# A hybrid state-space and attention layer on one core: early stages rebuilt around TensorE's queue, GpSimd adds squares, the scan spread

## What is computed

```python
mod = silu(c) @ w_ada + b_ada                 # shift1, scale1, gate1, shift2, scale2, gate2
hn = rmsnorm(x, norm_mix_pre) * (1 + sc1) + sh1
z, xbc, dt, q, k, v, gates = split(hn @ w_in)
y_ssm = grouped_rmsnorm(scan(silu(conv(xbc)), dt) * silu(z))       # 8 groups, chunked scan
y_att = attention(rope(q), rope(k), v)        # window of 128, 64 queries at a time, learned sinks
merged = sigmoid(g_ssm) * (y_ssm @ w_ssm_out) + sigmoid(g_att) * (y_att @ w_att_out)
x = x + g1 * rmsnorm(merged @ w_out, norm_mix_post)
gate, up = split((rmsnorm(x, norm_ffn_pre) * (1 + sc2) + sh2) @ w_ffn_in)
x = x + g2 * rmsnorm((silu(conv(gate)) * up) @ w_ffn_out, norm_ffn_post)
```

## Time and profile before

| | us |
|---|---|
| median of 3 runs | 1462.64 (1460.32 to 1465.84) |
| the profiled execution | 1468.68 |
| its span, first to last instruction | 1466.9 |
| stage A and the start of stage B, to the end of chunk 1 | 0 to 79.2 |
| the rest of stage B | 79.2 to 238.9 |
| the group loop | 238.9 to 709.3 |
| what follows | 709.3 to 1466.9 |
| TensorE busy | 1365.2 (93% of the span) |
| VectorE, ScalarE, GpSimd busy | 772.5, 502.6, 405.6 |

### The profile page before, as it was taken

How to read it: one execution, slowest core, us unless ns; L and a number is a source line. 1 busy time by engine, 2 the same in 40 slices (tenths; PEclk the granted TensorE clock), 3 DMA queues, 4 the chain that set the end, 5 groups by cost and what they waited for, 6 DMA issues and landing times. The chain is left out here.

```text
span 1466.9 us, 24764 instructions
## 1 busy us (share of the span) xinstructions
PE 1365.2 (93%) x10355; PEld 1269.8 (87%) x10355; DVE 772.5 (53%) x1288; ACT 502.6 (34%) x888; POOL 405.6 (28%) x263
## 2 busy tenths in 40 slices
PE   4699998999999999999899999994899999999994
PEld 1488987898898998988889999993899999999993
DVE  1644414877887888778353000328566666650114
ACT  2212424363553553634323222333333333322221
POOL 0532310101101011011123444331444444443332
PEclk7599987999999999999999999996799999999997
DMA  9276624344245343341333222221222222222221
GB/s 373 101 259 223 198 77 120 104 127 141 70 136 147 89 123 116 118 131 45 113 119 132 87 87 87 101 82 38 74 87 87 87 87 87 87 74 91 88 68 62
DMA packets 68351, 165.83 MB, mean 113 GB/s; under 512 B 21160, under 2 KB 34376, under 8 KB 64768
## 3 DMA queue, kind: packets, MB, share of 16 engines
q1 hardware_dynamic: 68240, 164.25, 34.7%
HBM read 150.85 MB, written 13.83 MB: 112 GB/s over the span
## 5 line engine op out<-in xcount | busy, mean ns | idle before, releaser
L181 PE MATMUL psum<-hp_hi,w_hi 128*128 128x274 f32 x1488 | 458.7, 308 | 15.9 <-POOL hp_lo L298 11.7
L159 POOL TENSOR_TENSOR w_lo<-raw_w,w_hi 128x1024 fp32r<-128x1024 f32 x127 | 307.0, 2418 | 569.8 <-ACT w_hi L153 569.8
L181 PE MATMUL psum<-hp_lo,w_hi 128*128 128x274 f32 x1488 | 438.6, 295 | 0.0
L181 PE MATMUL psum<-hp_hi,w_lo 128*128 128x274 f32 x1488 | 438.1, 294 | 0.0
L153 ACT ACTIVATE w_hi<-raw_w 128x1024 fp32r<-128x1024 f32 x175 | 185.1, 1058 | 629.4 <-PE psum L181 576.5
L181 PEld LDWEIGHTS psum<-hp_hi,w_hi 128*128 128x128 f32 x1488 | 287.8, 193 | 35.7 <-issue 16.4
L181 PEld LDWEIGHTS psum<-hp_lo,w_hi 128*128 128x128 f32 x1488 | 290.7, 195 | 0.8
L181 PEld LDWEIGHTS psum<-hp_hi,w_lo 128*128 128x128 f32 x1488 | 288.9, 194 | 0.0
L181 PE MATMUL psum<-hq_hi,w_hi 128*128 128x274 f32 x832 | 248.1, 298 | 15.4 <-POOL hq_lo L1568 13.3
L181 PE MATMUL psum<-hq_hi,w_lo 128*128 128x274 f32 x832 | 244.9, 294 | 0.0
L181 PE MATMUL psum<-hq_lo,w_hi 128*128 128x274 f32 x832 | 244.6, 294 | 0.0
(11 more groups left out here) (235 smaller groups left out, 2018.9 us busy)
## 6 DMA issues: line engine op xcount, KB each, us to landing
raw_w<-in_w_grp SPq DMA_DIRECT2D x57, 512.0 KB, 3.8
raw_w<-in_w_ffn_in SPq DMA_DIRECT2D x44, 512.0 KB, 3.6
ada<-in_w_ada SPq DMA_DIRECT2D x12, 1024.0 KB, 20.3
ada_g<-in_w_ada SPq DMA_DIRECT2D x6, 2048.0 KB, 8.6
raw_w<-in_w_ffn_out SPq DMA_DIRECT2D x22, 512.0 KB, 3.5
acs_b<-mem_acs SPq DMA_DIRECT2D x8, 1096.0 KB, 7.1
raw_w<-in_w_ssm SPq DMA_DIRECT2D x16, 512.0 KB, 3.5
raw_w<-in_w_qkv SPq DMA_DIRECT2D x13, 512.0 KB, 6.7
```

The source lines that it names most:

```text
L159: eng.tensor_tensor(flat(w_lo[self.hl_slot(n)]), raw_w[self.raw_slot(n)][:], flat(w_hi[self.hl_slot(n)]).bitcast(F32), ALU.subtract).then_ ...
L181: mm = pe.matmul(out[:, h, :], w, x[:, cols], start=first and j == 0, stop=last and j == 2)
```

## The change

Stage A. BLOCKS is now SHIFT1, SCALE1, SHIFT1 + 1, SCALE1 + 1, so that two blocks are enough for the first four tiles; the two blocks of SHIFT2 move to stage B. x is loaded first, in two halves, into mr (which is free then). After the sum, VectorE norms (`normed`) and makes hp_lo (`lower`) and w_lo; ScalarE scales and shifts (`scaled`) and makes hp_hi; GpSimd only clears constants. TensorE multiplies chunks 0 and 1 tile by tile between the blocks 2 and 3. The tables cos, sin, rot, gp and mask_u, chunks 3 and 4 of the weights and the block GATE1 are loaded at the end of stage A.

```diff
-                for t in range(2):
+                for t in range(len(src)):
                     mm = pe.matmul(psum[0:SUMW, bank, col + j:col + j + 1], src[t][:, c0:c0 + SUMW], ones[:, 0:1],
-                                   start=t == 0, stop=t == 1)
+                                   start=t == 0, stop=t == len(src) - 1)
...
+        MOD_BLOCKS = [GATE1, GATE1 + 1, SCALE2, SCALE2 + 1, SHIFT2, SHIFT2 + 1, GATE2, GATE2 + 1]
...
+            BLOCKS = [SHIFT1, SCALE1, SHIFT1 + 1, SCALE1 + 1]
+            ada = [ada_g1, *(sb(st, f"ada{n}", [P, KB, ADA_W]) for n in range(1, len(BLOCKS)))]
+            mod_row = late_row
+            x = mrg
...
+                    for n in range(2):
+                        ks = slice(KB // 2 * n, KB // 2 * (n + 1))
+                        sp.dma_start(x[:, ks, :], i["x"][:, ks, :]).then_inc(in_x[n], 16)
...
                         if n == 4:
-                            sp.dma_start(x[:], i["x"]).then_inc(in_x, 16)
+                            w.load(sp, 0)
+                            w.load(sp, 1)
...
-                        if a >= ADA_SLOTS:
-                            sp.wait_ge(ada_done, a - ADA_SLOTS + 1)
-                        sp.dma_start(ada[a % ADA_SLOTS][:, ks, :], i["w_ada"][BLOCKS[a], :, ks, :]).then_inc(in_ada[n], 16)
-                    for n in range(RAW_SLOTS):
-                        w.load(sp, n)
+                        sp.dma_start(ada[a][:, ks, :], i["w_ada"][BLOCKS[a], :, ks, :]).then_inc(in_ada[n], 16)
+                    w.load(sp, 2)
+                    for dst, name in ((cos, "cos"), (sin, "sin"), (rot, "rot"), (dt_par, "dt_par"), (gp_all, "gp"), (mask_u, "mask_u")):
+                        sp.dma_start(dst[:], i[name]).then_inc(in_s, 16)
+                    w.load(sp, 3)
+                    w.load(sp, 4)
+                    sp.wait_ge(ada_done, 1)
+                    sp.dma_start(ada_g1[:], i["w_ada"][MOD_BLOCKS[0]]).then_inc(ada_in[0], 16)
...
+                    def scaled(t):
+                        act.wait_ge(gain_s, t // 4 + 1)
+                        act.wait_ge(xr_s, t + 1)
+                        if t >= 2:
+                            act.wait_ge(lo_s, t - 1)
+                        for c0, L, g in RANGES:
+                            ins = act.activation(h[t % 2][:, c0:c0 + L], xr[t % 2][:, c0:c0 + L], ACT.Identity,
+                                                 bias=mod[:, t, g:g + 1], scale=gain[:, 0, t, g:g + 1])
+                        ins.then_inc(h_s, 1)
+                        act.wait_ge(h_s, t + 1)
+                        act.activation(hp_hi[:, t, :], h[t % 2][:], ACT.Copy).then_inc(hi_s, 1)
...
+                    act.activation(halves(rstd[:]), slot(1), ACT.Sqrt, bias=eps_c, scale=1.0 / D).then_inc(root_s, 1)
+                    row(0)
+                    row(1)
+                    w.split_hi(act, 0)
+                    act.wait_ge(const_s, 3)
+                    scaled(0)
+                    scaled(1)
+                    w.split_hi(act, 1)
+                    scaled(2)
+                    scaled(3)
+                    row(2)
+                    row(3)
+                    for t in range(4, KB):
+                        scaled(t)
+                    w.split_hi(act, 2)
...
+                    def normed(t):
                         if t >= 2:
...
+                            dve.wait_ge(h_s, t - 1)
+                        dve.tensor_tensor(xr[t % 2][:], x[:, t, :], rstd[:], ALU.mult).then_inc(xr_s, 1)
+
+                    def lower(t):
+                        dve.wait_ge(hi_s, t + 1)
+                        dve.tensor_tensor(hp_lo[:, t, :], h[t % 2][:], hp_hi[:, t, :].bitcast(F32), ALU.subtract).then_inc(lo_s, 1)
+
+                    normed(0)
+                    gains(0)
+                    normed(1)
+                    w.split_lo(dve, 0)
+                    for t in range(2, KB):
+                        lower(t - 2)
+                        normed(t)
+                        if t == 3:
+                            w.split_lo(dve, 1)
+                        if t == 5:
+                            gains(1)
+                    lower(KB - 2)
+                    lower(KB - 1)
+                    w.split_lo(dve, 2)
+                    dve.wait_ge(lo_s, KB)
...
+                    for a in range(2):
+                        turn_block(a)
+                    first_chunk(0)
+                    first_chunk(1)
+                    block_product(2)
+                    first_chunk(2)
+                    first_chunk(3)
+                    turn_block(2)
+                    second_chunk(0)
+                    block_product(3)
+                    second_chunk(1)
+                    second_chunk(2)
+                    turn_block(3)
+                    second_chunk(3)
+                    for k in range(4, KB):
+                        first_chunk(k)
+                        if k == KB - 2:
+                            second_chunk(4)
+                    for k in range(5, KB):
+                        second_chunk(k)
+                    w.block = 2 * KB
...
+                            if n == AT + 3:
+                                sp.wait_ge(v_s, 2)
...
+                                load_attention(sp, at.in_s, S, at.q, scratch["qs"], scratch["ks"], scratch["vs"][0:WIN, :], scratch["vs"][WIN:WIN + S, :],
...
+                            if n - 4 in MOD_AT[0:6]:
+                                load_ada(sp, (2, 3, 4, 5, 7, 6)[MOD_AT.index(n - 4)])
...
-                            w.split_hi(act, n + 2)
                             if n == AT + 1:
                                 at.exps(act, 0)
+                            if n >= 1:
+                                w.split_hi(act, n + 2)
...
+                                    at.evac_turned(act, 0, 2)
                                 if n == AT + 2:
-                                    at.evac_turned(act, 0, 2)
...
-                                if n == AT + 1 and k == 1:
+                                if n == AT + 1 and k == 2:
                                     pe.wait_ge(tok_s, 1)
-                                    pe.wait_ge(row_s, 6)
...
+                                    pe.wait_ge(row_s, 8)
+                                if n == AT + 1 and k in (2, 4):
+                                    for kv in (k - 2, k - 1):
                                         at.scores(pe, 0, kv)
-                                u = (n - AT - 2) * KB + k - 3
+                                u = (n - AT - 2) * KB + k - 6
...
+                                if u == 8:
+                                    for a in range(2):
+                                        mm = turn_rows(pe, 6, 8 * a, late_row[:, 2 + a, :])
+                                    mm.then_inc(turn_s, 1)
+                            for j in (() if n < 2 or n > QK else (0, 1) if n == 2 else (n - 1,)):
...
+                            pool.wait_ge(ysq_s, g + 1)
+                            pool.tensor_tensor(y_sq[:, 0, :], y_sq[:, 0, :], y_sq[:, 1, :], ALU.add).then_inc(ysq2_s, 1)
...
+                            at.exps(act, g)
+                            w.split_hi(act, GT * g + 2)
                             act.wait_ge(ysum_s, g + 1)
                             act.activation(ss_all[:, :, g:g + 1].rearrange("p a b -> p (a b)"), psum[0:SUMW, 6, 256:256 + 2 * SUMT],
                                            ACT.Copy)
-                            at.exps(act, g)
-                            w.split_hi(act, GT * g + 2)
...
                             diff(c)
+                            expand(c)
                             diff(c + 1)
-                            expand(c)
...
-                            pe.wait_ge(ysq_s, g + 1)
+                            fill(2)
+                            pe.wait_ge(ysq2_s, g + 1)
                             pe.wait_ge(at.se_s, KV * (g + 1))
-                            token_sums(pe, 6, 256, (y_sq[:, 0, :], y_sq[:, 1, :])).then_inc(ysum_s, 1)
-                            fill(9)
+                            token_sums(pe, 6, 256, (y_sq[:, 0, :],)).then_inc(ysum_s, 1)
+                            fill(7)
...
-                            scan(c)
-                            turn_scores(c + 2)
-                            fill(3)
-                            scan(c + 1)
...
-                            scan(c + 4)
-                            fill(3)
+                            for d in range(NC5):
+                                outputs(c + d)
+                                fill(1)
+                                end_state(c + d)
+                                if d + 2 < NC5:
+                                    turn_scores(c + d + 2)
+                                fill(2)
```

291 lines of the change are left out of this document (134 added, 157 removed).

## The result

| | before | after |
|---|---|---|
| median | 1463.39 us (1460.32 to 1465.84) | 1428.22 us (1426.60 to 1432.43) |
| profiled execution, its span | 1468.68, 1466.9 | 1426.60, 1424.8 |
| clock granted, mean of that execution | 0.946 | 0.973 |
| chunk 2 starts | 79.2 | 56.28 |
| loop starts | 238.91 | 205.83 |

The account below looks back on a forecast made before the run. TensorE's one long queue bounds the kernel, with idle and half clock ahead of the loop. 31.4 us ahead of the loop plus 9.8 in it gave 41.2: 1427.5 from the profiled execution, 1421.4 from the median, range 1408 to 1440.

Parts of the forecast that it names:

- Stage A: Up to the start of chunk 2 of the QKV stream: from 79.2 to about 58 us, gain 21 us, 16 to 25.
- the rival of half clock from 30 us on: Stage A: idle between tiles keeps TensorE at half clock, chunk 2 starts at 63 to 65, 1427 to 1429; chance 0.15.
- Stage B: From chunk 2 to the loop's first instruction: 149.5 us instead of 159.7, bounds 147 and 156.
- The loop: Group loop: 9.8 us less, from 8 for shorter column sums, 2.6 of clock, less 0.8 of waits; bounds 3 and 13.
- a push of 1.6 fits in: 0 in my sum: Loop: GpSimd's add may delay VectorE by 1.6 us, but scores have 1.7 us to spare before their turn; cost 0.
- the wait for the state: Loop's scan: TensorE's wait for h_p grows by 0.1 us a group through later end_state, 0.8 in all.
- against the median I forecast 1421.4: Whole kernel: the 41.2 us gain taken from the median 1462.64, 6.0 below the profiled execution, instead of from 1468.68.
- The late data: Stage B: attention loads or a w_ada block 2 to 5 us late and the clock falls, gain 30, 1433; chance 0.1.
- the add that isn't hidden: Loop: GpSimd's add starts behind VectorE, column sums 1.5 us late in each group, 12 us, 1436; chance 0.1.
- the state's chain: Loop's scan: later end_state delays five pieces, 3.9 us a group, plus 10 at half clock: 1533, slower; chance 0.03.
- the change that does nothing: Stages ahead of the loop: barrier still holds the loads or stages wait elsewhere, only the loop gains, 1453; chance 0.03.
- the case of more than forecast: Stage A: full clock all through, chunk 2 at 54, time 1412 to 1416; chance 0.09.

Follow-up runs that it names:

- turn_four: The changed kernel, but all four late w_ada rows turned at once behind the first turn of the sample's scores, as before: 1431.50 us, 0.976 of before.
- loop_only: The kernel before, with only the change's edits to token_sums and the group loop: 1458.71 us, 0.995 of before.
- norm_first: The changed kernel, but VectorE normalises the second turn's scores ahead of its lower weight half in the loop: 1425.18 us, 0.972 of before.
- scan_whole: The changed kernel, but each piece's end state directly behind its outputs again, three tiles in a row behind both: 1425.64 us, 0.974 of before.
- stages_only: The change's stages ahead of the loop, with the group loop as before the change: 1433.71 us, 0.980 of before.
- two_sums: The changed kernel without GpSimd's add, so column sums take both halves of the squares, 24 matmuls a group: 1437.19 us, 0.982 of before.
- late_two: late_halves without GpSimd's add, so with 24 matmuls in each group's column sums: 1426.74 us, 0.973 of before.
- the two halves timed alone: stages_only and loop_only, each carrying one part of the change against the kernel before: 1433.71 us (0.980) and 1458.71 us (0.995).
- tiles_dve_pool: The changed kernel, but chunk tiles' scale and shift on VectorE and their lower half on GpSimd again: 1435.08 us, 0.979 of before.
- late_halves: norm_first, and the sixth weight chunk's lower half put behind the update of the carried state: 1417.46 us, 0.967 of before.

## Why the prediction was right, and what it missed

**Stage A: 56.28 for 58.** The order of events is the one forecast, and the column sum came at 16.18 for 16.1. The first tile was ready at 28.5, not at 30.7, since the first gains were there at 25.8. A tile took ScalarE 1.7 us (42.15 to 43.87), not 1.5: scale and shift of the two sequences are 1.12 us together, not 0.8. TensorE ran at half clock from 28.3 to 31.7 and from 45.4 to 52.2 us, but at full clock in between, so the rival of half clock from 30 us on fell.

**Stage B: 149.55 for 149.5.** Waits of 0.78 us at chunk 3 (0.5 forecast) and 2.07 at the barrier (1.9); one of 0.56 ahead of the sample's second turn that I hadn't seen; no fall of the clock. So the 1 us that I put down for half clock at the start didn't come, and the other waits took its place: that the sum is right to 0.1 is luck, the order of events is not. The loads for the attention were in time. turn_four shows that the four blocks in a row can make the clock fall, as I held, but loop_only shows that the depth of it in the profile of before was that execution's.

**The loop: 5.5 for 9.8, the mis-sized term.** The column sums became 0.99 us shorter a group, as forecast (1.0), and the two tiles moved ahead of them took away some 0.15 us at their start. The add was hidden: GpSimd ended at 388.74, 0.69 us ahead of the sums at 389.43 (forecast 0.5).

```profile
387.36 1.38 POOL L1048 TENSOR_TENSOR cv<-cv 128x548 f32<-128x548 f32 x1 [17.14 <-ACT cv L1108]
...
389.43 1.06 PE L236 MATMUL psum<-ones,cv 128*92 128x1 f32 x12
```

Two steps then took away 0.7 us a group: 0.41 that norm_first gave back and 0.31 that scan_whole did. The first is "a push of 1.6 fits in: 0 in my sum". I took the room ahead of the turns from the group at 305 us in the earlier trace rows, 2.7 us. In that group the clock had fallen behind the sums (its length is 59.5), so TensorE came 1.5 us late there; and I looked at the first turn only. In a group of before at full clock the room ahead of the first turn is 1.2 us, and the scores of the second turn, which stand behind a weight half, are ready 0.8 us ahead of it (431.97 + 0.54 against 433.31):

```profile
430.37 0.55 DVE L498 TENSOR_SCALAR sc<-sc,rden 128x192 f32<-128x192 f32 x2
430.83 1.22 DVE L159 TENSOR_TENSOR w_lo<-raw_w,w_hi 128x1024 fp32r<-128x1024 f32 x1
431.97 0.54 DVE L498 TENSOR_SCALAR sc<-sc,rden 128x192 f32<-128x192 f32 x2
...
432.12 0.27 PE L508 MATMUL psum<-ident,sc 128*128 128x128 f32 x1
...
433.31 0.27 PE L508 MATMUL psum<-ident,sc 128*128 128x128 f32 x1
```

With TensorE 1 us earlier they are late: 0.41 a group. No push by GpSimd was needed for it. The second is the wait for the state, 0.1 forecast and 0.28 found. The copy of the state at the second piece did wait for the later end_state (0.84 us idle at 418.60, none before), and less of it was made good than I thought. In sum, from the first to the last column sums: seven groups of 0.36 are 2.5 us, two falls of the clock that were missing 3.1, and the late first turn of the first group costs 1.1. The rest, 1.0, lies at the loop's two ends, most of it in the clock up to the first column sums (0.71 in before, 0.82 in after):

```profile
238.90:247.80 8.90, 8.89 (x52) 7.99 (x53) 7.79 (x14) 5.65 (x7) 0.31 (x2) 0.71 0.76 234
205.80:215.50 9.70, 9.67 (x66) 8.88 (x66) 8.52 (x15) 5.68 (x7) 2.21 (x3) 0.82 0.79 238
```

So some 4 of the 5.5 us are clock. The part at the entry differs between executions of one code. Whether the 3.1 us behind it belong to the change stays open: both profiles of the old loop have such falls (two in before, one in stages_only, each a group of 59.5 us), and from the second group on none of the twelve of the new loop and its variants has one. The number of one-column products alone isn't the reason, since two_sums and late_two have all 24 of them and no fall.

**Past the loop: 3.5 for 0.** The code is the same. The profiled executions of all these kernels took 753.8 to 762.7 us there, so the 3.5 us lie within that scatter and are no gain that I can show.

**The base: the largest part of the miss.** Between the profiles the forecast gain of 41.2 stands against 42.1 measured. That closeness is in part luck: ahead of the loop the change gave 1.7 us more than forecast and in the loop 4.3 less, and the 3.5 past it, which nobody forecast and the change doesn't touch, made up for most of that. Between medians it stands against 35.2, and the forecast of 1421.4 is 6.8 us low. The step that failed is "against the median I forecast 1421.4". It took the excess of the profiled execution, 6.0 us, for something that both kernels would have. But the profile of after was 1.6 us under its median, and that of before was an execution at the lowest clock. A good part of its excess, as I read it, lay where the change takes the half clock away, at the end of stage B (0.61 in the earlier trace rows; with 0.82 loop_only started its loop 4.0 us earlier on the same code). How much too large the sum is for a usual execution is known only roughly: the two halves timed alone give 29.9 us (0.980 of 1466.3) and 6.9 (0.995) by the ratios of the table, together 36.8, and 32.6 and 7.6, together 40.2, by the difference of their medians to 1466.33.

**The rivals.** The late data, the add that isn't hidden, the state's chain and the change that does nothing all fell; so did the case of more than forecast, chunk 2 at 54 us at full clock. VectorE wasn't held by the add. Its reduction of the scores, which runs beside it from 387.90 to the add's end at 388.74, took 1.75 us before, where GpSimd was silent, and after:

```profile
423.09 1.75 DVE L472 TENSOR_REDUCE mx<-sc 128x8 f32<-128x1536 f32 x1
```

```profile
387.90 1.75 DVE L560 TENSOR_REDUCE mx<-sc 128x8 f32<-128x1536 f32 x1
```

The Trainium skill (SBUF — State Buffer, Who interferes with whom) says that a VectorE reduction never contends with GpSimd on this chip, and that an instruction with two inputs in SBUF contends with a GpSimd instruction that reads SBUF. Both halves of that agree with rows here: the reduction at 1.75, and the norm at 1.87 instead of 0.72 in tiles_dve_pool.

## To carry to other kernels

When one engine is made faster, list for each thing it waits for how early that thing is now, in a stretch at full clock, and for every consumer, not the first of a kind. What is less early than the saving becomes the new wait, and the cure may be as cheap as putting work that nobody wants yet (here a weight half) behind work that is wanted. And a profile is one execution: its time over the median sits in certain stretches, and a change that removes just these can gain less on the median than in that profile.

## What the runs showed of the hardware

- A wait cost TensorE more than the idle that its row shows: 0.18 us of idle was worth 0.41 us when it was removed (after, norm_first), and 0.99 us was worth 1.07 (norm_first, late_halves).
- The same instructions are granted different clocks from one execution to the next: the end of stage B ran at 0.64 and at 0.82 (23.8 and 10.1 us at half clock), and what lies past the loop took from 753.8 to 762.7 us with the same code.
- In turn_four the clock fell to half 2.5 us into a row of 32 products of two columns, with no wait ahead of them, and stayed there for 20.4 us. The one profiled execution shows it; the times of the other three speak against so long a fall.
